# Sums of squares in column groups, decode scores in two banks, adaLN pieces between chunks

## The reference

```python
mod = silu(c) @ w_ada + b_ada                 # adaLN: shift, scale, gate for each group and sequence
# layer 0: a Conformer convolution module
h = rmsnorm(x) * (1 + scale) + shift
a, gate = split(h @ w_a_in)
u = a * sigmoid(gate)
u = causal_depthwise_conv(u, width=31)
u = layernorm(u)                              # mean, then sum of squares of what is centred
y = silu(u) @ w_a_out
...
# layer 1: stick-breaking attention, 16 heads of 64; keys and values of the decode sequences
# lie in 4 pages of 128 tokens each, found through page_table
z = q @ k.T / 8 + bias
log_1m = where(causal, log_sigmoid(-z), 0)
suffix = reverse_cumsum(log_1m) - log_1m
att = where(causal, exp(log_sigmoid(z) + suffix), 0)
o = att @ v
```

## Time and profile before

| | us |
|---|---|
| median of 3 runs | 1504.09 |
| lowest and highest | 1502.54, 1505.28 |
| the profiled execution | 1502.1 |
| its span in the profile | 1500.5 |
| TensorE busy in the span | 1460.8 |
| VectorE, ScalarE, GpSimd busy | 979.5, 909.1, 269.2 |

### The profile page before, as it was taken

The page is one execution under the profiler, slowest core; times in us unless marked ns, Lnnn a source line. Parts: engine busy times, 40 slices in busy tenths (PEclk is TensorE's granted clock), DMA queues, the critical chain, the costliest instruction groups (busy, mean ns, idle before and its releaser), DMA issues.

```text
span 1500.5 us, 28447 instructions
## 1 busy us (share of the span) xinstructions
PE 1460.8 (97%) x11276; PEld 1349.6 (90%) x11276; DVE 979.5 (65%) x1475; ACT 909.1 (61%) x1658; POOL 269.2 (18%) x469
## 2 busy tenths in 40 slices
PE   5999999999999999999999989999999999999998
PEld 4777659999999999999889856679999999999997
DVE  4799966878744878645546356664887754767643
ACT  4699877777643776535435556654767643666633
POOL 2488810000000332100000022210000000322200
PEclk9999999999999999999999999999999999999999
DMA  9887683345554454653337366653255554454653
GB/s 381 304 292 281 250 282 127 95 161 170 187 176 141 157 165 161 196 172 127 127 105 260 113 225 225 226 198 117 84 171 169 172 181 153 144 168 167 196 166 101
DMA packets 72117, 273.50 MB, mean 182 GB/s; under 512 B 8064, under 2 KB 10128, under 8 KB 71600
## 3 DMA queue, kind: packets, MB, share of 16 engines
q1 hardware_dynamic: 65824, 247.69, 48.7%
q0 software_dynamic: 5872, 23.64, 4.6%
q10 hardware_dynamic: 288, 0.35, 0.1%
HBM read 262.80 MB, written 8.85 MB: 181 GB/s over the span
## 4 chain that ended last, share of the span: by engine, by line
PE 83%; DVE 10%; ACT 4%; issue 2%; DMA 0%; POOL 0%; DVEq 0%; SPq 0%; ACTq 0%
PE ps L736 65%; DVE ps L1879 4%; PE ps L987 3%; PE ps L713 3%; PE ps L1059 1%; PE ps L1065 1%; PE ps L1042 1%; PE ps L1126 1%; PE ps L1078 1%; PE ps L1093 1%; PE ps L792 1%; DVE w_lo L1710 1%; DVE y L1996 1%; PE ps L902 1%; ACT w_att L1614 1%
## 5 line engine op out<-in xcount | busy, mean ns | idle before, releaser
L736 PE MATMUL ps<-h_hi,w_hi 128*128 128x288 f32 x1920 | 570.9, 297 | 3.8 <-DVE w_lo L1710 2.1
L736 PE MATMUL ps<-h_lo,w_hi 128*128 128x288 f32 x1920 | 565.3, 294 | 0.0
L736 PE MATMUL ps<-h_hi,w_lo 128*128 128x288 f32 x1920 | 565.3, 294 | 0.0
L1710 DVE TENSOR_TENSOR w_lo<-raw,w_hi 128x1024 fp32r<-128x1024 f32 (+1 forms) x296 | 387.3, 1310 | 228.5 <-ACT w_hi L1270 228.2
L1270 ACT ACTIVATE w_hi<-raw 128x1024 fp32r<-128x1024 f32 (+1 forms) x309 | 347.0, 1124 | 106.4 <-PE ps L736 73.1
L736 PEld LDWEIGHTS ps<-h_hi,w_hi 128*128 128x128 f32 x1920 | 360.1, 188 | 10.4 <-DVE h_lo L1784 4.3
L736 PEld LDWEIGHTS ps<-h_lo,w_hi 128*128 128x128 f32 x1920 | 360.1, 188 | 1.1 <-issue 0.2
L736 PEld LDWEIGHTS ps<-h_hi,w_lo 128*128 128x128 f32 x1920 | 360.0, 188 | 0.0
L736 PE MATMUL ps<-act_hi,w_hi 128*128 128x288 f32 x704 | 208.4, 296 | 0.0
L736 PE MATMUL ps<-act_lo,w_hi 128*128 128x288 f32 x704 | 207.7, 295 | 0.0
L736 PE MATMUL ps<-act_hi,w_lo 128*128 128x288 f32 x704 | 207.0, 294 | 0.0
(11 more groups left out here) (265 smaller groups left out, 2075.8 us busy)
## 6 DMA issues: line engine op xcount, KB each, us to landing
raw<-w_k_dram SPq DMA_DIRECT2D x245, 512.0 KB, 3.5
raw<-w_down_dram SPq DMA_DIRECT2D x64, 704.0 KB, 4.1
ada_w<-w_ada_dram SPq DMA_DIRECT2D x71, 512.0 KB, 6.3
k_page<-cache_kt_dram SPq DMA_DIRECT2D x32, 512.0 KB, 5.2
v_page<-cache_v_dram POOLq DMA_DIRECT2D x32, 512.0 KB, 5.1
ada_h<-w_ada_dram SPq DMA_DIRECT2D x7, 512.0 KB, 6.2
ada_u<-w_ada_dram SPq DMA_DIRECT2D x6, 512.0 KB, 15.0
ada_g<-w_ada_dram SPq DMA_DIRECT2D x6, 512.0 KB, 6.0
```

The costliest lines, as they stand in the source:

```text
L736: mm = pe.matmul(ps[:, BANK[b], 0:HALF], lhsT=w[s][:, kb * P:(kb + 1) * P], rhs=v[:, at, :] if down else v[:, at, lo:hi], start=(at == 0 a ...
L1710: dve.tensor_tensor(w_lo[s][:, 0:cols], raw[n % RING][:, 0:cols], w_hi[s][:, 0:cols].bitcast(F32), ALU.subtract).then_inc(s_lo, 1)
```

## The change

1. *First stage.* In quarters 0 and 1 the pieces of quarter q+2 go between the products of chunk q and those of chunk q+4, and the transposing matmul goes between the two blocks of chunk q+4. ScalarE loads the table with the sigmoid ahead of its first use.
2. *Sums of squares.* `square_sum` multiplies with `sum_w` (128x32, all 1/32) into one of four groups of 32 output partitions, the groups taken in turn; each group gets two of the eight chunks. Then ScalarE copies the four partial sums to SBUF and one matmul with `mean_w` adds them (`square_total`). All 32 partitions of a group hold the same sum, so 1/32 and 1/1024 give the mean.
3. *Decode scores.* Two pages' scores stay in bank 7, the other two go to bank 6, which they share with the pairs' output; TensorE's loop has the second half behind the last suffix matmuls. The copies with the bias move from ScalarE to VectorE, one for each half. `k_used` counts halves, and what waits for it (SyncE, GpSimd, the last splits) waits for the second. At the head of the loop `pair_o(0)` moves ahead of `softplus_lo` on VectorE.
4. *Transposes.* `turn_scores` and `turn_output` use TensorE's transposing mode; the output's transposes write 128 columns each instead of 64.

```diff
@@ -436,7 +437,8 @@
         sig = place("sig", [P, TT], at=(at := temp(shared)))
-        odd_taps = place("odd_taps", [P, TP], at=at)
+        sq_part = place("sq_part", [P, HALF], at=[at[0], at[0] + TP * 4])
+        at[0] += TP * 4
         mod_t = place("mod_t", [P, 4 * P], at=at)
@@ -483,6 +485,7 @@
         o_seq = place("o_seq", [P, 2 * P], at=behind_raw(1))
+        sum_w = place("sum_w", [P, 32], at=behind_raw(2))
         q_seq = place("q_seq", [P, PAIRS, 4 * TS], at=behind_raw(2))
@@ -501,7 +504,7 @@
-        STAT, MEAN_BANK, TAP_BANK = 2, (0, 3), 1
+        STAT, MEAN_BANK, TAP_BANK, SCORE_BANK = 2, (0, 3), 1, (7, 6)
@@ -670,10 +674,10 @@
             for i in range(1, NS):
-                sp.wait_ge(k_used, i)
+                sp.wait_ge(k_used, 2 * i)
                 for t in range(PAGES):
                     page_load(sp, i, t, k_page, cache_kt, k_in)
-            sp.wait_ge(k_used, NS)
+            sp.wait_ge(k_used, 2 * NS)
             for n in range(O_LOAD + 2, LOADS):
@@ -850,13 +854,16 @@
                 pe.wait_ge(first_seq_low, q + 1)
-                for kb in (q, q + C // 2):
-                    norm_wait(0, kb, None)
-                    both_halves(0, kbs=(kb,))
-                    both_halves(1, kbs=(kb,))
+                norm_wait(0, q, None)
+                both_halves(0, kbs=(q,))
+                both_halves(1, kbs=(q,))
                 if q + 2 < QUARTERS:
                     first_pieces(q + 2)
+                norm_wait(0, q + C // 2, None)
+                both_halves(0, kbs=(q + C // 2,))
+                if q + 2 < QUARTERS:
                     first_turn(q + 2)
+                both_halves(1, kbs=(q + C // 2,))
@@ -899,9 +906,16 @@
                 for j in range(2):
-                    mm = pe.matmul(ps[:, 2 * STAT + h, 0:HALF], lhsT=mean_w[:], rhs=pair[:, j, :],
-                                   start=(p + j == 0), stop=(p == C // 2 - 1 and j == 1))
+                    t = (2 * p + j) % 4
+                    mm = pe.matmul(ps[32 * t:32 * t + 32, 2 * STAT + h, 0:HALF], lhsT=sum_w[:], rhs=pair[:, j, :],
+                                   start=(p < 2), stop=(p >= 2), skip_group_check=True)
                 mm.then_inc(sq_used, 1)
+            def square_total(h):
+                pe.wait_ge(sq_copied, h + 1)
+                pe.matmul(ps[:, 2 * STAT + h, 0:HALF], lhsT=mean_w[:], rhs=sq_part[:], start=True, stop=True)\
+                    .then_inc(sq_total, 1)
@@ -911,8 +925,10 @@
             late_pieces(ADA_RING)
+            pe.wait_ge(sum_w_made, 1)
             for p in range(C // 2):
                 square_sum(0, p)
+            square_total(0)
             mean_sum(C - 1, 1)
@@ -944,6 +960,7 @@
                     late_pieces(2)
+            square_total(1)
@@ -1080,27 +1097,32 @@
-            def seq_scores(i):
-                pe.wait_ge(q_staged, 4 * i + 4)
-                if i > 0:
-                    pe.wait_ge(seq_bank_free, i)
-                for t in range(PAGES):
+            def seq_scores(i, part):
+                if part == 0:
+                    pe.wait_ge(q_staged, 4 * i + 4)
+                    if i > 0:
+                        pe.wait_ge(seq_bank_free, i)
+                else:
+                    pe.wait_ge(pair_bank_free, max(i, 1))
+                for n in range(PAGES // 2):
+                    t = PAGES // 2 * part + n
                     pe.wait_ge(k_in[t], 16 * i + 16)
                     for a in range(2):
                         for j in range(4):
                             p = 2 * j + a
-                            mm = pe.matmul(ps[32 * j:32 * j + 32, 7, t * PAGE:(t + 1) * PAGE], lhsT=q_seq[:, p, :],
-                                           rhs=k_page[t][:, p * PAGE:(p + 1) * PAGE], start=(t == 0 and a == 0),
-                                           stop=(a == 1), skip_group_check=True)
+                            mm = pe.matmul(ps[32 * j:32 * j + 32, SCORE_BANK[part], n * PAGE:(n + 1) * PAGE],
+                                           lhsT=q_seq[:, p, :], rhs=k_page[t][:, p * PAGE:(p + 1) * PAGE],
+                                           start=(n == 0 and a == 0), stop=(a == 1), skip_group_check=True)
                 mm.then_inc(k_used, 1)
             def turn_scores(i):
-                pe.wait_ge(seq_z_copied, i + 1)
                 for c in range(4):
+                    if c % 2 == 0:
+                        pe.wait_ge(seq_z_copied, 2 * i + c // 2 + 1)
                     mm = pe.matmul(ps[:, 7, c * P:(c + 1) * P], lhsT=z_seq[:, c * P:(c + 1) * P], rhs=ident_f[:],
-                                   start=(c == 0), stop=True, skip_group_check=True)
+                                   start=(c == 0), stop=True, is_transpose=True, skip_group_check=True)
                 mm.then_inc(seq_turned, 1)
@@ -1130,10 +1152,10 @@
                 pe.wait_ge(seq_o_copied, i + 1)
-                columns = ident_f[:].rearrange("p (j a b) -> p j a b", a=2, b=2 * TS)
                 for a in range(2):
-                    mm = pe.matmul(ps[:, 7, 256 + 64 * a:320 + 64 * a], lhsT=o_seq[:, a * P:(a + 1) * P],
-                                   rhs=columns[:, :, a], start=(a == 0), stop=True, skip_group_check=True)
+                    at = 256 + a * (P - 2 * TS)
+                    mm = pe.matmul(ps[:, 7, at:at + P], lhsT=o_seq[:, a * P:(a + 1) * P],
+                                   rhs=ident_f[:], start=(a == 0), stop=True, is_transpose=True, skip_group_check=True)
                 mm.then_inc(seq_o_turned, 1)
@@ -1188,7 +1210,8 @@
             pe.wait_ge(new_step, 8)
-            seq_scores(0)
+            seq_scores(0, 0)
+            seq_scores(0, 1)
             turn_scores(0)
@@ -1198,7 +1221,8 @@
             turn_output(0)
-            seq_scores(1)
+            seq_scores(1, 0)
+            seq_scores(1, 1)
             turn_scores(1)
@@ -1211,8 +1235,9 @@
                 suffix_part(1, i, False)
-                seq_scores(i)
+                seq_scores(i, 0)
                 suffix_part(1, i, True)
+                seq_scores(i, 1)
                 turn_scores(i)
@@ -1350,6 +1375,7 @@
             split(2)
+            act.preload_act_table_set(SIGMOID)
@@ -1427,6 +1453,8 @@
                 act.wait_ge(sq_used, (h + 1) * (C // 2))
+                act.activation(sq_part[:], ps[:, 2 * STAT + h, 0:HALF], ACT.Copy).then_inc(sq_copied, 1)
+                act.wait_ge(sq_total, h + 1)
                 act.activation(rs[:, lo:hi], ps[:, 2 * STAT + h, 0:HALF], ACT.Ln, bias=eps_col[:, 0:1]).then_inc(a_ln, 1)
@@ -1618,11 +1646,6 @@
-            def seq_copy(i):
-                act.wait_ge(k_used, i + 1)
-                act.activation(z_seq[:], ps[:, 7, :], ACT.Identity, bias=bsb_row[:]).then_inc(seq_z_copied, 1)
@@ -1658,10 +1681,8 @@
             first_exp(1, 1)
-            act.wait_ge(bias_row, 1)
             ln(0, 1)
             ln(1, 1)
-            seq_copy(0)
             softplus_hi(0, 1)
@@ -1669,7 +1690,6 @@
             weights(1, 1)
-            seq_copy(1)
             seq_exp(1)
@@ -1682,11 +1702,10 @@
                 weights(0, i)
-                seq_copy(i)
                 weights(1, i)
                 seq_exp(i)
                 seq_ln(i)
-            act.wait_ge(k_used, NS)
+            act.wait_ge(k_used, 2 * NS)
             split(KEY_SLOT_LOAD)
@@ -2157,7 +2176,7 @@
                         r = slice(HD * j, HD * j + HD)
-                        src = ps[r, 7, 256:384].rearrange("p (a t h q) -> p t a h q", a=2, h=2, q=TS)[:, :, :, j]
+                        src = ps[r, 7, 256:512].rearrange("p (a t g h q) -> p t a g h q", a=2, g=2, h=2, q=TS)[:, :, :, 0, j]
                         hi, low = (h[r, :, TP + i * TS:TP + (i + 1) * TS].rearrange("p (t a) q -> p t a q", a=2)
@@ -2174,6 +2193,14 @@
+            def seq_copy(i):
+                for part in range(2):
+                    half = slice(TP // 2 * part, TP // 2 * (part + 1))
+                    dve.wait_ge(k_used, 2 * i + part + 1)
+                    dve.tensor_scalar(z_seq[:, half], ps[:, SCORE_BANK[part], 0:TP // 2], bsb_row[:], None, ALU.add)\
+                        .then_inc(seq_z_copied, 1)
@@ -2212,13 +2240,15 @@
             softplus(1, 1)
+            pair_o(0)
+            seq_copy(0)
             softplus_lo(0, 1)
             softplus_lo(1, 1)
-            pair_o(0)
             seq_cap(0)
             seq_max(0)
             seq_o_copy(0)
             seq_o(0)
+            seq_copy(1)
             seq_cap(1)
@@ -2232,9 +2262,10 @@
                 pair_o(i - 1)
+                seq_copy(i)
                 seq_cap(i)
                 seq_max(i)
-            dve.wait_ge(k_used, NS)
+            dve.wait_ge(k_used, 2 * NS)
             split(KEY_SLOT_LOAD)
@@ -2256,6 +2287,7 @@
             pool.memset(four_diag[:], 1.0).then_inc(s_const, 1)
+            pool.memset(sum_w[:], 1.0 / 32).then_inc(sum_w_made, 1)
             pool.wait_ge(s_const, 9)
@@ -2447,7 +2479,7 @@
             for i in range(1, NS):
```

(5 more changed lines are left out.)

## The result

The changed kernel takes 1506.73 us (median of 17 executions, 1505.35 to 1508.6), the kernel before 1503.69 on the same chip (17 executions, 1501.4 to 1505.28): 3.0 us longer, ratio 1.0023 with a 95% interval of 1.0017 to 1.0029. The forecast was 1501.6, in a range from 1499.3 to 1504.8. The profiled execution took 1506.4 us with a span of 1504.8, 4.3 longer than before.

A forecast was written before the change was run, and what follows sets the result against it. TensorE, busy 1460.8 of 1500.5 us, was taken as the bound. Terms -1.7 (first stage), +1.65 (LayerNorm), -2.45 (rounds), +0.25 (head), -0.25 (last turned output) sum to -2.5: from 1504.09 to 1501.6 us, range 1499.3 to 1504.8.

The forecast's parts named there:

- Rival C: TensorE's clock falls behind new waits: one fall gives 1503.3 us, one in each of six rounds 1511.8; chance 0.10.
- the new wait before 226.7: LayerNorm, second half: TensorE idles near 2.8 us before restarting; one clock fall there gives -0.8, 1503.3 us.
- rival B: Attention loop: the split gains only 0.24 us a round, the head loses 0.7; -0.5, 1503.6 us; chance 0.15.
- First stage, -1.7: Moving pieces and transposing matmuls earlier starts the last quarter's chunk at 41.65 instead of 43.35, 1.7 us gained.
- The pieces' transfers set no floor: First stage: all sixteen pieces' transfers, 12 MB with those queued ahead, arrive by 33 us; the last are wanted at 35.
- handed on whole: First stage: whatever TensorE gains before 46.7 us reaches the later stages undiminished.
- LayerNorm, first half: Matmuls two at a time in column groups start the logarithm and VectorE's centring 0.3 us sooner; 0.3 us gained.
- second half, +1.65: LayerNorm: closing sum behind the last pieces delays the logarithm to 222.8 and TensorE's restart to 226.7; 1.65 us lost.
- Attention rounds, -0.49 each: Scores in two banks shorten each round from 19.3 to 18.8 us, 2.45 us gained over five rounds.
- Head of the loop, +0.25: Sequence 0's second half waits for its bank, 1.65 us later; sequence 1 gives most back, leaving 0.25 us lost.
- Last turned output, -0.25: Cheaper transposes of the output, two records instead of four, gain 0.25 us once at the end.
- Nothing in the loop: Attention loop: the cheaper turned output gains nothing there, as the suffix matmuls behind it start when `sp_lo` is just finished.

The follow-up runs named there:

- kernel with the old head: Changed kernel with sums of squares as before and sequence 0 as before (four pages in bank 7, ScalarE copy, VectorE's order): 1498.82 us, ratio 0.9975.
- the squares alone: Kernel before with only the sums of squares on column groups added, nothing else of the change: 1506.64 us, ratio 1.0024.
- the squares with the wait filled: Kernel before with the sums of squares on column groups, plus ten added matmuls in TensorE's 3.15 us wait: 1505.68 us, ratio 1.0016.
- the pieces alone: Kernel before with only the first stage's pieces put between its chunks and the early sigmoid table load: 1502.15 us, ratio 0.9992.
- the groups in the first half: Kernel with the old head, plus sums of squares on column groups in the LayerNorm's first half only: 1499.34 us, ratio 0.9973.
- true transposes alone: Kernel before with only TensorE's true transposes in place of products with the identity, for scores and outputs: 1503.43 us, ratio 0.9999.
- the split alone: Kernel with the old head (pieces, scores in two banks, VectorE copies), but turns as products with the identity: 1501.38 us, ratio 0.9989.

## Why the prediction was wrong

*What failed.* The step that failed first is the price of TensorE's new waits: each was counted at its length, and the clock behind it at nothing. Rival C, the falls of the clock, had a chance of 0.10, and its cost was not in the sum. It named "the new wait before 226.7" and the waits of the rounds. The first did bring a fall; the rounds, with their six transposes, kept the full clock. The longest new wait is in the prediction's own numbers and in no rival: at the head of the loop the scores started at 868.52 in the kernel before, and two pages take 1.0 us, while the working has "the bank at 873.8", over 4 us later.

```profile
868.52 1.96 PE L1093 MATMUL ps<-k_page,q_seq 128*32 128x128 f32 x64
```

Both long waits brought a fall, +1.5 and +0.8 us, shown by filling them. With these two the sum of -2.5 would have been -0.2. The rest of the way, against the profile, is the first stage and the rounds, whose gains were put 1.2 and 0.9 us too high, the LayerNorm's 0.4, the 0.2 by which sequence 1 gave less, and the fall at `z_pair(1)`, 1.7 us. The range had room for one fall at most, and its upper end is not what it names: rival B and one fall are -0.5 + 1.7 = +1.2, that is 1505.3 before any scatter. The measured 1506.73 lies above either.

*First stage, -1.7.* The mechanism is right up to 42 us: 42.11 instead of 43.35 in a profile that was 0.4 late in starting. Behind it 1.1 us are left by the fourteen profiles, and 0.9 by the medians (whose interval also holds none). The failing sentences are "The pieces' transfers set no floor", which was worked out for the first sixteen pieces and not for the four before the second block, and "handed on whole". Those four took 1.86 us from start to start before (46.72 to 48.58) and take 2.47 now, waiting for their weights, so 0.6 us of the 1.24 are gone there.

*LayerNorm, first half.* 0.3 forecast, 0.16 measured.

*LayerNorm, second half, +1.65.* The logarithm was to start at 222.8 and TensorE at 226.7; they started at 222.67 and 226.59. That these times agree is luck: the forecast's are counted from a stage that starts as before, and in this profile the stage starts 0.5 us sooner. From the first mean matmul to the restart the loss is 2.0 us. The chain was right: the restart is 3.92 us behind the logarithm, where 3.93 was taken. The missing 0.4 are in three sizes: 0.14 in the first half, 0.12 in the pairs (0.68 saved up to the closing sum, 0.8 taken), 0.09 between the closing sum and the logarithm. A pair costs 0.61 us with 0.20 in the products behind, 0.81 in place of 0.97, where 0.77 was taken. By the prediction's estimate its columns alone are 0.48, so going into column groups and back carries 0.33. The Trainium skill (TensorEngine Tiling (Array Packing), Key Properties) says that a change of tiling mode drains TensorE. The 0.33 us fit that; how much of them is the drain no run here shows.

*Attention rounds, -0.49 each.* They gave -0.31 each, in the four rounds from `z_pair` to `z_pair` and in the round behind sequence 1. The scores in two parts take 2.03 us instead of 1.88, and the split turn, from its first record to `z_pair`, 1.04 instead of 1.58. The two transposes cost 0.37, near the 0.3 taken. There is an idle time of 0.24 before the last two and none at `z_pair`, as said. Rival B (0.24 a round) was nearer than the forecast.

*Head of the loop, +0.25.* At the full clock it is near: the wait puts `z_pair(2)` 1.58 us later (1.65 forecast), and sequence 1 gives 1.14 back (1.36 forecast). From `z_pair(2)` to `z_pair(3)` 1.44 us go, but 0.30 of them belong to the round behind sequence 1. The kernel with the old head has the same 25.29 us there, so the forecast set a gain that stands alone against a loss that could be left out.

*Last turned output, -0.25.* It gave -0.22 (0.66 us before, 0.44 after). *Nothing in the loop* was right: the suffix behind the turned output waits 0.24 us for `sp_lo`.

*Fall at `z_pair(1)`.* Five of the fourteen profiles have it, with about 4.1 us for `z_pair(1)`: the changed kernel, the squares alone, the squares with the wait filled, the pieces alone, and the groups in the first half. The other nine have 2.43. The code and the wait before it (0.59 us) are the same in all, and the pieces alone and the squares alone, which have no edit in common, both have it. Why it comes in some executions stays open, and so does how often the changed kernel has it. That matters, because it is 1.7 of the profile's 4.3 us.

## What to carry to other kernels

List every wait that a change adds to TensorE where it is the bound, with its length. Price each at the wait plus what the low clock may cost behind it, which was 0.8 and 1.5 us for the two waits here. The longest one stood in the working, and only its effect on the next wait was counted. An edit that takes work from the bound engine and adds a step (copy, closing sum) to a chain that it will wait for pays only where the chain has slack. In the first half it was neutral, in the second it cost 2.2 us from the first chunk of `a_out` to the restart. And edits on two alternating limits must be tried together: true transposes alone and the split alone each left the round as it was, within 0.03 us.

## What the runs showed of the hardware

- TensorE fell to 1.2 GHz behind every wait of the fourteen profiles, from 30 us on, that was longer than 1.9 us: 4.13 (three profiles), 3.15 (two), 2.23, 1.95 and 1.93 us. Behind the wait of 1.67 us at the first chunk of `a_out`, which all fourteen have (1.67 or 1.68), it fell in one. The wait of 0.77 us before block 19 brought no fall, but `z_pair(1)`, behind a wait of 0.59 us and small matmuls (64x64 and one row), had one in five. So the length of the last wait alone does not decide. The two long waits, when filled with matmuls, brought none. The Trainium skill (TensorE: Matmul & The Clock Gate, Terms) takes the penalty as the throttled time times the share of pulses left out. For 227.3 to 230.7 that is an estimate of 1.7 us, and the filled wait shows 1.55.
- In thirteen of the fourteen profiles the first products of 25 to 30 us run partly at the low clock too; the one with the squares alone did not. Its first stage ended 2 us sooner than in the kernel before, yet its second block started only 1.0 us sooner, because the pieces waited for their weights.
- An fp32 transpose of 128x128 leaves one record of TensorE, the product with the identity two. Read from start to start, the cost depends on what follows: two transposes took 0.37 us ahead of `z_pair` and 0.20 ahead of a projection, four products 1.10 us with `z_pair` behind them (its wait taken off) and 0.86 ahead of a projection.
